# A trunk kernel whose mixer trips are reordered, with the residual's scaling on ScalarE

## The chip, the core and the metric

The kernel runs on one core of a Trainium2 chip. The metric is the device time of one execution in microseconds. Time before: 2114.56 us, the median of 3 runs (2111.04 to 2116.69).

## The reference, cut to what matters

Two decoder layers of 1024 tokens by 1024 channels in float32. Layer 0 has a pooling and gating mixer, layer 1 (the "odd" one) a short gated convolution. Each is followed by a residual, a layer norm, a feed-forward block of width 4096, another residual and norm, and a gated embedding.

```python
def short_conv_mixer(x, w_in, conv_w, w_out):
    proj = jnp.einsum('bsd,de->bse', x, w_in)
    gate_b, gate_c, h = jnp.split(proj, 3, axis=-1)
    z = gate_c * h
    zp = jnp.pad(z, ((0, 0), (CONV_WIDTH - 1, 0), (0, 0)))
    conv = sum(conv_w[k] * zp[:, k:k + s] for k in range(CONV_WIDTH))   # width 3
    return jnp.einsum('bse,ed->bsd', gate_b * conv, w_out)

x = layer_norm(DEEPNORM_ALPHA * x + mix, ln1_g[i], ln1_b[i])
```

## The kernel before, in words

Every product of float32 matrices is done as three matmuls of rounded parts (high by high, high by low, low by high), so each operand has to be split before: ScalarE copies the high part, GpSimd or VectorE subtracts it from the value for the low part. Large products are also done by a seven-product scheme on 2 x 2 quarters (Winograd's form of Strassen's scheme), so sums and differences of quarters are needed besides.

The order of the work is one list, made in `make_plan` (L338). Each engine walks through this list and does its own part of each stage, in order; semaphores join them. An instruction that waits thus holds all that stands behind it on its engine, and the same goes for SyncE, which issues nearly all DMAs.

The odd layer's mixer is laid out by `short_conv` (L558). Its parts, in order:

- Slab "c" and slab "h": the first 256 channels of gate_c and of h, by plain products. Each slab's weights lie in four pieces in `raw`, are loaded by SyncE and split (`split_high` on ScalarE, `split_low` on GpSimd, L1246). The split of slab "h" is part of stage "c". While TensorE works on "c", the second half of the tokens is turned and split. GpSimd can start with the trips' operands only after the slab, and the weights of the first trip (`w1_raw`) are loaded where `raw` lay, once it is split. At the end of stage "h" (L2168) VectorE forms z = c * h and does the convolution of block 0: four quarters by three operations.
- Ten trips, each of seven products (A11, S1, S2, A12, S4, S3, A22) of 12 matmuls: block 0 of gate_b, then for each of the blocks 1 to 3 the trips c, h and b. A22 of a trip is done within the next one, behind its S1; the last trip has S3 ahead of S4. The operand of step i + 4 is made during step i: sums S1 and S3 by VectorE (L1903, L1906), S2 and S4 by GpSimd (L1326, L1333), high parts by ScalarE (L1525), low parts by GpSimd (L1260). GpSimd makes the low parts of S1 and of S2 only when it comes to S2 and S4 of its own order.
- `od_evictions` (L1734) is VectorE's reading of the products: names such as c22 (final sum of a quarter), m22 (z's quarter, gated), g22 (the mixer's value), h1 to h4 (sums of quarters for the product with w_out). `od_conv` (L1713) is the convolution of one quarter: a scaling by the third tap, then two multiply-adds, each waiting for the one before. Before, two quarters follow S4 and two follow A22 of each trip h. TensorE may enter A22 only once S3's sum (L1787) is formed from the same bank.
- `od_copies` (L1409) is ScalarE's part. `od_loads_and_spills` (L1044) issues the weights' loads, writes the b trips' values to memory (`spill_g`), and `load_od_item` (L995) reads them back.
- 14 items: the product of the mixer's values with w_out, seven forms of two items of 24 matmuls each. An item is prepared (`prep`, L1483 and L1984) by splitting its values (hop) and its weights (wop). VectorE makes weight sums (`wsum`, L1955) where a form needs them, one item ahead. After the second item of a form VectorE adds the banks to the residual (L2010, L2013); the next form that uses the same banks waits for it.
- The residual is scaled by 4 ** 0.25 in eight pieces, one in each of eight trips, by GpSimd (stage "alpha", L1289).

Of the kernel before, what the change touches and what calls it, by code (L numbers as in the profile page):

```python
# [63 lines left out]
OD_HOP_AT = (184, 192, 48, 52, 128, 132, 200, 48, 52, 128, 132, 200, 48, 52)  # L64
OD_W_AT = (188, 196, 32, 36, 168, 172, 176, 180, 184, 188, 32, 36, 168, 172, 176, 180, 32, 36)
OD_STEPS = dict(
    c=dict(S1=("s15",), A22=("c21",), S2=("u1",), A12=(), S4=("c12",), S3=("c22",)),
    h=dict(S1=("s15",), A22=("c21", "m21", "v100", "v101", "v102", "v110", "v111", "v112"), S2=("u1",), A12=("m11",),
           S4=("c12", "m12", "v000", "v001", "v002", "v010", "v011", "v012"), S3=("c22", "m22")),
    b=dict(S1=("s15",), A22=("c21", "g21", "h4"), S2=("u1",), A12=("g11",), S4=("c12", "g12"),  # L70
           S3=("c22", "g22", "h1", "h2", "h3")))
OD_LAST = dict(OD_STEPS["b"], S3=("c22", "g22"), S4=("c12", "g12", "h1", "h2", "h3"))
# [81 lines left out]
class Ahead:  # L154


    def __init__(self, layer, after, items, pairs, joined):
        self.layer, self.items, self.pairs, self.joined = layer, items, pairs, joined
        n = len(items)
# [3 lines left out]
        self.act = [base["act"] + 2 * i + 2 for i in range(n)]  # L163
        self.first_load = [sum(len(FORMS[form][2]) for form, _ in items[:i]) for i in range(n)]
        loads = sum(len(FORMS[form][2]) for form, _ in items)
        dve, taken = base["dve"], base["taken"]
        self.sum, self.hop_low, self.dve, self.taken = [None] * n, [], [], []
        for i in range(-1, n):
            if i + 1 < n:
                dve += FORMS[items[i + 1][0]][3]  # L170
                self.sum[i + 1] = dve
            if i >= 0:
                self.hop_low.append(dve + 1)
                dve += 2
                self.dve.append(dve)
                taken += items[i][1] < pairs - 1 and not (joined and i == n - 2)
                self.taken.append(taken)
        self.total = dict(act=base["act"] + 2 * n, dve=dve, taken=taken, pool=base["pool"] + pairs,
                          hop=base["hop"] + n, load=base["load"] + loads)

# [72 lines left out]
class Trips:  # L253
# [6 lines left out]
    def __init__(self, layer, after, end):  # L260
# [19 lines left out]
        for b, op in self.seq:  # L280
# [8 lines left out]
            if layer == OD:  # L289
                kind = OD_TRIPS[b - PLAIN][0]  # L290
                for name in (OD_STEPS[kind] if b < end - 1 else OD_LAST).get(op, ()):
                    self.step[b, name] = len(self.step) + 1
# [5 lines left out]
            if op in self.QUARTER:  # L298
                self.quarter[b, self.QUARTER[op]] = layer * 4 * blocks + len(self.quarter) + 1
        self.total = dict(ops=base["ops"] + n, sums=base["sums"] + 2 * blocks, moves=base["moves"] + blocks,  # L300
                          loads=base["loads"] + blocks // 2)

# [2195 lines left out]
```

## Time and profile before

| | us |
|---|---|
| median of 3 runs | 2114.56 (2111.04 to 2116.69) |
| the profiled execution | 2113.19 |
| its span, first to last instruction | 2111.6 |
| TensorE busy | 2067.5 (98%) |
| VectorE busy | 1328.9 (63%) |
| ScalarE busy | 835.3 (40%) |
| GpSimd busy | 810.8 (38%) |

The mixer of the odd layer lies from 1000 to 1350 us. Matmuls overlap, so the time of one row (391 ns) is longer than the distance from one start to the next. The number in brackets behind an instruction is how long its engine stood idle before it, and what ended that.

### The profile page before, as it was taken

The numbers are of one execution on the slowest core, as the hardware profiler recorded it, in microseconds if no ns is written. First come the engines' busy times: TensorE is split into PE (matmuls) and PEld (weight loads), VectorE is DVE, ScalarE is ACT, GpSimd is POOL, SyncE is SP. The second block draws the span as 40 slices with busy tenths as digits, with TensorE's granted clock in tenths as the row PEclk, the third lists the DMA queues.
The fourth block names the chain that finished last, engine by engine and source line by source line (L and its number), as shares of the span: only waits on it lengthen the run. The fifth ranks groups of instructions, "written<-read, shape, count | busy, mean of one in ns | idle before, by whom it ended". The sixth has DMA issues, their size and how long they took to land. (4 is left out here: it accounts for less than half of the span.)

```text
span 2111.6 us, 25132 instructions
## 1 busy us (share of the span) xinstructions
PE 2067.5 (98%) x9437; PEld 1712.4 (81%) x9437; DVE 1328.9 (63%) x1689; ACT 835.3 (40%) x1215; POOL 810.8 (38%) x533
## 2 busy tenths in 40 slices
PE   9999999999999999999899997999999999999999
PEld 9888788888888888888777776888888888888887
DVE  4744775556666666565567757676565566666663
ACT  3112554544544335531322223554544543334530
POOL 5113167777512000230666650157777512000220
PEclk9999999999999999999999998999999999999999
DMA  5111024434599554310022229024444499554221
GB/s 186 41 60 55 26 80 155 151 139 160 189 366 376 199 189 160 110 56 15 20 96 88 72 76 340 28 81 151 142 146 164 177 366 387 184 196 170 95 85 40
DMA packets 191252, 307.10 MB, mean 145 GB/s; under 512 B 13504, under 2 KB 71964, under 8 KB 191132
## 3 DMA queue, kind: packets, MB, share of 16 engines
q1 hardware_dynamic: 190432, 305.19, 41.7%
q8 instruction: 75, 1.23, 0.2%
q14 instruction: 45, 0.37, 0.1%
q10 hardware_dynamic: 700, 0.31, 0.1%
HBM read 234.14 MB, written 71.30 MB: 145 GB/s over the span
## 5 line engine op out<-in xcount | busy, mean ns | idle before, releaser
L1246 POOL TENSOR_TENSOR w_lo<-raw,w_hi 128x512 fp32r<-128x512 f32 x92 | 140.7, 1561 | 736.3 <-ACT w_hi L1354 736.3
L1495 ACT CAST hop_hi<-h_raw 128x1024 fp32r<-128x1024 f32 x126 | 132.5, 1051 | 290.7 <-PE bank_a L2234 165.3
L1525 ACT CAST op_hi<-op_sum 128x512 fp32r<-128x512 f32 x152 | 94.5, 622 | 369.8 <-POOL op_sum L1333 97.6
L1260 POOL TENSOR_TENSOR op_lo<-op_sum,op_hi 128x512 fp32r<-128x512 f32 x152 | 222.5, 1480 | 42.6 <-ACT op_hi L1525 36.6
L2232 PE MATMUL bank_a<-wop_hi,hop_hi 128*128 128x512 f32 x576 | 225.3, 391 | 8.0 <-DVE resid L2010 8.0
L1988 DVE TENSOR_TENSOR hop_lo<-h_raw,hop_hi 128x1024 fp32r<-128x1024 f32 x126 | 154.4, 1226 | 121.8 <-ACT hop_hi L1495 121.5
L2234 PE MATMUL bank_a<-wop_hi,hop_lo 128*128 128x512 f32 x576 | 225.0, 391 | 0.0
L2233 PE MATMUL bank_a<-wop_lo,hop_hi 128*128 128x512 f32 x576 | 225.0, 391 | 0.0
L1260 POOL TENSOR_TENSOR op_lo<-w_raw,op_hi 128x512 fp32r<-128x512 f32 x114 | 165.0, 1447 | 120.5 <-ACT op_hi L1525 119.1
L2232 PE MATMUL bank_a<-xt_hi,op_hi 128*128 128x512 f32 x456 | 178.3, 391 | 1.8 <-DVE b L1752 1.8
L2233 PE MATMUL bank_a<-xt_lo,op_hi 128*128 128x512 f32 x456 | 178.1, 391 | 0.0
L2234 PE MATMUL bank_a<-xt_hi,op_lo 128*128 128x512 f32 x456 | 178.0, 390 | 0.0
L2232 PE MATMUL bank_b<-wop_hi,hop_hi 128*128 128x512 f32 x432 | 169.5, 392 | 3.2 <-DVE wop_lo L1991 3.2
L2234 PE MATMUL bank_b<-wop_hi,hop_lo 128*128 128x512 f32 x432 | 168.8, 391 | 0.0
L2233 PE MATMUL bank_b<-wop_lo,hop_hi 128*128 128x512 f32 x432 | 168.8, 391 | 0.0
L2232 PE MATMUL bank_a<-xt_hi,w_hi 128*128 128x512 f32 x320 | 127.6, 399 | 6.4 <-POOL w_lo L1246 6.4
L2232 PEld LDWEIGHTS bank_a<-wop_hi,hop_hi 128*128 128x128 f32 x576 | 108.8, 189 | 30.8 <-DVE wop_lo L1991 8.4
L1991 DVE TENSOR_TENSOR wop_lo<-w_raw,wop_hi 128x1024 fp32r<-128x1024 f32 x108 | 132.6, 1228 | 0.6
L2233 PEld LDWEIGHTS bank_a<-wop_lo,hop_hi 128*128 128x128 f32 x576 | 108.8, 189 | 22.7
L2234 PEld LDWEIGHTS bank_a<-wop_hi,hop_lo 128*128 128x128 f32 x576 | 108.7, 189 | 22.8
L1287 POOL TENSOR_TENSOR w_raw<-w_raw,w_raw 128x1024 f32<-128x1024 f32 x18 | 44.3, 2461 | 213.7 <-DMA w_raw<-in_ffn_w_dram 181.2
L2232 PE MATMUL bank_b<-t_hi,op_hi 128*128 128x512 f32 x304 | 120.4, 396 | 5.0 <-POOL op_lo L1260 4.9
(239 smaller groups left out, 4970.1 us busy)
## 6 DMA issues: line engine op xcount, KB each, us to landing
w_raw<-in_ffn_w_dram SPq DMA_DIRECT2D x144, 512.0 KB, 6.8
h_raw<-h_spill SPq DMA_DIRECT2D x112, 512.0 KB, 5.5
h_spill<-h_tile SPq DMA_DIRECT2D x170, 256.0 KB, 2.2
w_raw<-in_ffn_w_dram SPq DMA_DIRECT2D x112, 256.0 KB, 3.3
w_raw<-in_od_w_in_dram SPq DMA_DIRECT2D x40, 256.0 KB, 3.4
w_raw<-in_od_w_out_dram SPq DMA_DIRECT2D x18, 512.0 KB, 6.7
raw<-in_ple_gate_w_dram SPq DMA_DIRECT2D x32, 256.0 KB, 3.5
h_spill<-h_tile2t SPq DMA_DIRECT2D x28, 256.0 KB, 2.0
```

The lines of the kernel that those rows point to most:

```text
L1246: pool.tensor_tensor(lo, raw[:, n % NRAW, :], hi.bitcast(F32), ALU.subtract).then_inc(lo_split, 1)
L1260: pool.tensor_tensor(by_four(op_lo[s]), by_four(src) if src is not None else w1_quarter(b, op), by_four(op_hi[s]).bitcast(F32), ALU.subtra ...
L1287: pool.tensor_tensor(w2_chunk(a, i), w2_chunk(a, i), w2_chunk(a, i, 1), ALU.subtract)\
L1495: act.copy(hop_hi[k][:, :, :], h_raw[a.hop_chunk(i)][:, :, :]).then_inc(ahead_hi, 1)
L1525: act.copy(by_four(op_hi[s]), src).then_inc(op_high, 1)
L1988: dve.tensor_tensor(hop_lo[k][:, :, :], h_raw[a.hop_chunk(i)][:, :, :], hop_hi[k][:, :, :].bitcast(F32), ALU.subtract).then_inc(ahead_dve, 1)
L1991: dve.tensor_tensor(wop_lo[k][:, :, :], w2_source(a, i), wop_hi[k][:, :, :].bitcast(F32), ALU.subtract).then_inc(ahead_dve, 1)
L2232: pe.matmul(dst, s_hi, m_hi, start=first, stop=False, skip_group_check=on_top)
L2233: pe.matmul(dst, s_hi, m_lo, start=False, stop=False, skip_group_check=on_top)
L2234: return pe.matmul(dst, s_lo, m_hi, start=False, stop=last, skip_group_check=on_top)
```

## The change

Slab "h" is split by a stage of its own ("split") at the start of the mixer, ahead of the turned units. The convolution of a quarter keeps two operations on VectorE; the first, the scaling by the third tap, is done by ScalarE (`last_tap`). The four quarters' convolutions are spread over the steps S4 of trip h and A11, S2 and A12 of trip b; those of block 0 lie in the first trips and no longer in stage "h". The sums h2 and h3 and their writing to memory go to step A11 of the next trip. The last block's g11 and g21 are not written to memory: items 2 and 3 read them from their tiles, with two pieces of a copy and of a subtraction each. Items 1, 2 and 3 are loaded earlier (at S1 and S3 of the last trip), from other places. In the mixer a weight sum is made right before its own item (`sum_lead` false). "alpha" is ScalarE's in the mixer's trips.

```diff
-OD_HOP_AT = (184, 192, 48, 52, 128, 132, 200, 48, 52, 128, 132, 200, 48, 52)
-OD_W_AT = (188, 196, 32, 36, 168, 172, 176, 180, 184, 188, 32, 36, 168, 172, 176, 180, 32, 36)
+OD_HOP_AT = (184, 48, 52, 192, 128, 132, 200, 48, 52, 128, 132, 200, 48, 52)
+OD_W_AT = (188, 32, 36, 196, 168, 172, 176, 180, 184, 188, 32, 36, 168, 172, 176, 180, 32, 36)
+OD_DIRECT = {2: "g11", 3: "g21"}
...
-        if n + 1 < len(ahead[layer].items):
+        if not ahead[layer].sum_lead:
+            add("wsum", item=n, layer=layer)
+        elif n + 1 < len(ahead[layer].items):
             add("wsum", item=n + 1, layer=layer)
         add("prep", item=n, layer=layer)
...
     def short_conv():
         tr, a = trips[OD], ahead[OD]
+        add("split")
         turn = turns("gate", 1, list(range(KT)), ring="B", nested=True)
-        add("c", slab=("od", D), half=0, paced=True, split_next=True, inner=[turn])
+        add("c", slab=("od", D), half=0, paced=True, split_next=False, inner=[turn])
...
-                elif i == 1:
-                    sp.wait_ge(od_step, tr.step[last - 1, "v112"])
-                elif i in (2, 3):
+                elif i in (1, 2):
                     sp.wait_ge(trip_done, tr.done[last, "A11"])
+                elif i == 3:
+                    sp.wait_ge(od_step, tr.step[last, "v102"])
...
                 if (b, op) == (last, "A11"):
                     load_od_item(0)
-                if (b, op) == (last - 1, "A22"):
+                if (b, op) == (last, "S1"):
                     load_od_item(1)
-                if (b, op) == (last, "A12"):
                     load_od_item(2)
+                if (b, op) == (last, "S3"):
+                    load_od_item(3)
                 if (b, op) == (last, "S4"):
                     load_od_item(4)
                 if (b, op) == (last, "A22"):
-                    for n in (3, 5, 6):
-                        load_od_item(n)
+                    load_od_item(5)
+                    load_od_item(6)
...
+                def last_tap(k, half):
+                    c = ROW_CONV + 2 * KT + blk * BT + k
+                    act.activation(cv_at(k, half, blk), z_at(k, half), ACT.Copy, scale=cols[:, c:c + 1])\
+                        .then_inc(od_tap, 1)
+
+                if kind == "h" and op == "S4":
+                    act.wait_ge(od_step, tr.step[b, "m11"])
+                    last_tap(0, 0)
+                if kind == "h" and op == "S3":
+                    act.wait_ge(od_step, tr.step[b, "m12"])
+                    last_tap(0, 1)
...
+                if kind == "b" and blk and op == "A11":
+                    act.wait_ge(od_step, tr.step[b - 1, "m22"])
+                    last_tap(1, 1)
+                if kind == "b" and blk and op == "S2":
+                    act.wait_ge(od_step, tr.step[b - 1, "m21"])
+                    last_tap(1, 0)
...
+                    if a.parts(i) == 2:
+                        act.copy(hop_hi[k][:, 0, :], h_raw[a.hop_chunk(i)][:, 0, :]).then_inc(ahead_hi, 1)
+                        act.wait_ge(od_step, trips[OD].step[trips[OD].end - 1, OD_DIRECT[i]])
+                        act.copy(hop_hi[k][:, 1, :], kept_of(i)).then_inc(ahead_hi, 1)
...
+                if st.kind == "alpha" and st.layer == OD:
+
+                    half = st.turned[st.tiles[0] // HT]
+                    act.wait_ge(sem_of[half[0]], half[1])
+                    for t in st.tiles:
+                        act.activation(resid[:, t, :], resid[:, t, :], ACT.Copy, scale=ALPHA).then_inc(acc_ready, 1)
...
-                dve.tensor_scalar(d, z_at(k, half), taps[2], None, ALU.mult).then_inc(od_step, 1)
-                od_wait(b, name + "0")
+                dve.wait_ge(od_tap, 4 * blk + {(0, 0): 1, (0, 1): 2, (1, 1): 3, (1, 0): 4}[k, half])
                 dve.scalar_tensor_tensor(out=d, in0=z_at(k, half, 1), scalar=taps[1], in1=d, op0=ALU.mult, op1=ALU.add)\
                     .then_inc(od_step, 1)
...
+                if op == "A11":
+                    if kind == "c" and blk == 1:
+                        od_conv(b - 1, 0, 1, 0)
+                    if kind == "c":
+                        od_other_sums(b - 1)
+                    if kind == "b":
+                        od_conv(b, blk, 0, 1 if blk else 0)
...
                     if kind == "h":
                         od_wait(b, "c12")
                         dve.tensor_tensor(q12, q12, cv_12[:, :], ALU.mult).then_inc(od_step, 1)
-                        od_wait(b, "m12")
-                        od_conv(b, blk, 0, 0)
-                        od_conv(b, blk, 0, 1)
+                        od_conv(b + 1, blk, 0, 0)
...
                     if kind == "h":
                         od_wait(b, "c21")
                         dve.tensor_tensor(q21, q21, cv_at(1, 0, blk), ALU.mult).then_inc(od_step, 1)
-                        od_wait(b, "m21")
-                        od_conv(b, blk, 1, 0)
-                        od_conv(b, blk, 1, 1)
```

## Rows read from the trace of the kernel before

**Rows 1.** The page: busy time, TensorE's granted clock in slices, one costliest group.
```profile
PE 2067.5 (98%) x9437; PEld 1712.4 (81%) x9437; DVE 1328.9 (63%) x1689; ACT 835.3 (40%) x1215; POOL 810.8 (38%) x533
...
PEclk9999999999999999999999998999999999999999
...
L1246 POOL TENSOR_TENSOR w_lo<-raw,w_hi 128x512 fp32r<-128x512 f32 x92 | 140.7, 1561 | 736.3 <-ACT w_hi L1354 736.3
```

**Rows 2.** Waits of TensorE, whole span: us in total, times, longest.
```profile
PE bank_a L2232 <- DVE resid L2010: 8.0, 1, 8.0
PE bank_b L2232 <- DVE z L1787: 6.6, 3, 3.1
PE bank_a L2232 <- POOL w_lo L1246: 6.4, 1, 6.4
PE bank_b L2232 <- POOL op_lo L1260: 4.9, 10, 3.4
PE bank_a L2232 <- POOL op_lo L1260: 3.9, 3, 1.8
PE bank_b L2232 <- DVE wop_lo L1991: 3.2, 1, 3.2
PE bank_a L2232 <- DVE b L1752: 1.8, 1, 1.8
```

**Rows 3.** Windows of 50 us: busy (x instructions) by engine, granted clock, DMA.
```profile
400.00:450.00 50.00, 49.83 (x220) 40.83 (x220) 32.63 (x35) 22.89 (x41) 40.66 (x28) 1.00 0.43 153
...
1050.00:1100.00 50.00, 46.33 (x196) 37.37 (x195) 38.42 (x42) 12.23 (x20) 29.36 (x20) 0.97 0.31 101
...
1300.00:1350.00 50.00, 44.03 (x183) 36.27 (x184) 42.01 (x63) 23.93 (x30) 8.19 (x5) 0.90 0.49 173
```

**Rows 4.** Timelines around slab "h": start, us, engine, line, operation.
```profile
941.28 10.48 SPq L933 DMA_DIRECT2D raw<-in_od_w_in_dram  x8
...
1009.40 0.92 DVE L1666 CAST xt_hi<-t_raw 128x512 fp32r<-128x512 f32 x2 [5.91 <-ACT t_raw L1405]
...
1015.88 12.28 POOL L1246 TENSOR_TENSOR w_lo<-raw,w_hi 128x512 fp32r<-128x512 f32 x1 [64.52 <-ACT w_hi L1354]
...
1032.91 0.63 PE L2234 MATMUL bank_a<-xt_hi,w_lo 128*128 128x512 f32 x1
```

**Rows 5.** Timelines, first trip b: VectorE behind S4 of h, TensorE at A22.
```profile
1114.87 1.40 DVE L1717 TENSOR_SCALAR cv<-z,cols 128x512 f32<-128x512 f32 x1
1116.31 0.75 DVE L1719 SCALAR_TENSOR_TENSOR cv<-z,cols,cv 128x512 f32<-128x512 f32 x1
1117.09 1.66 DVE L1722 SCALAR_TENSOR_TENSOR cv<-z,cols,cv 128x512 f32<-128x512 f32 x1
...
1124.20 0.79 PE L2232 MATMUL bank_b<-xt_hi,op_hi 128*128 128x512 f32 x1 [3.13 <-DVE z L1787]
```

**Rows 6.** Groups of instructions, 1000 to 1345 us; ScalarE's from 1340 to 1420.
```profile
L1722 DVE SCALAR_TENSOR_TENSOR cv<-z,cols,cv 128x512 f32<-128x512 f32 x12 | 14.4, 1200 | 0.4
...
L1294 POOL TENSOR_SCALAR resid<-resid 128x1024 f32<-128x1024 f32 x8 | 10.0, 1256 | 0.7
...
L1402 ACT ACTIVATE t_raw<-bank_b,cols 128x512 f32<-128x512 f32 x4 | 2.9, 779 | 0.4 <-PE bank_b L2271 0.4
```

**Rows 7.** Timelines, last trip: VectorE's S3 sum, TensorE at S2.
```profile
1248.74 0.68 DVE L1906 TENSOR_TENSOR op_sum<-w_raw 128x512 f32<-128x512 f32 x1
...
1254.55 0.77 PE L2232 MATMUL bank_b<-t_hi,op_hi 128*128 128x512 f32 x1 [3.38 <-POOL op_lo L1260]
```

**Rows 8.** Waits of SyncE's DMA queue, 1225 to 1325 us.
```profile
SPq L1017 <- DVE cv L1722: 20.1, 1, 20.1
```

**Rows 9.** Timelines, items 4 to 6: GpSimd's weight difference, VectorE's additions.
```profile
1292.42 2.36 POOL L1287 TENSOR_TENSOR w_raw<-w_raw,w_raw 128x1024 f32<-128x1024 f32 x1 [8.96 <-DMA w_raw<-in_od_w_out_dram]
...
1305.15 2.47 DVE L2010 TENSOR_TENSOR resid<-resid,bank_a 128x512 f32<-128x512 f32 x4
...
1317.92 2.46 DVE L2010 TENSOR_TENSOR resid<-resid,bank_a 128x512 f32<-128x512 f32 x4
```

More of the change, by code:

```diff
@@ L158, in __init__ @@
         self.layer, self.items, self.pairs, self.joined = layer, items, pairs, joined
+        self.sum_lead = layer != OD
         n = len(items)
@@ L172, in __init__, with parts @@
             if i >= 0:
-                self.hop_low.append(dve + 1)
-                dve += 2
+                if not self.sum_lead:
+                    dve += FORMS[items[i][0]][3]
+                    self.sum[i] = dve
+                self.hop_low.append(dve + self.parts(i))
+                dve += self.parts(i) + 1
                 self.dve.append(dve)
+                act += self.parts(i) + 1
+                self.act.append(act)
                 taken += items[i][1] < pairs - 1 and not (joined and i == n - 2)
                 self.taken.append(taken)
-        self.total = dict(act=base["act"] + 2 * n, dve=dve, taken=taken, pool=base["pool"] + pairs,
+        self.total = dict(act=act, dve=dve, taken=taken, pool=base["pool"] + pairs,
                           hop=base["hop"] + n, load=base["load"] + loads)
+    def parts(self, i):
+        return 2 if self.layer == OD and i in OD_DIRECT else 1
     def user_before(self, i):
@@ L301, in __init__, with gate_trip, od_names, conv @@
                           loads=base["loads"] + blocks // 2)
+    @staticmethod
+    def gate_trip(blk):
+        return PLAIN + OD_TRIPS.index(("b", blk))
+    def od_names(self, b, op):
+        kind, blk = OD_TRIPS[b - PLAIN]
+        last = b == self.end - 1
+        names = [(b, n) for n in dict(S1=("s15",), A22=("c21",), S2=("u1",), S4=("c12",), S3=("c22",)).get(op, ())]
+        def conv(owner, k, half):
+            names.extend((owner, f"v{k}{half}{tap}") for tap in (1, 2))
+        if kind == "c" and op == "A11":
+            if blk == 1:
+                conv(b - 1, 1, 0)
+            names += [(b - 1, "h2"), (b - 1, "h3")]
+        if kind == "h":
+            names += [(b, n) for n in dict(A22=("m21",), A12=("m11",), S4=("m12",), S3=("m22",)).get(op, ())]
+            if op == "S4":
+                conv(b + 1, 0, 0)
+        if kind == "b":
+            names += [(b, n) for n in dict(A22=("g21", "h4"), A12=("g11",), S4=("g12",), S3=("g22",)).get(op, ())]
+            if op == "A11":
+                conv(b, 0, 1 if blk else 0)
+            if op == "S2":
+                conv(b, 1 if blk else 0, 1)
+            if op == "A12":
+                conv(b, 1, 0 if blk else 1)
+            if op == ("S4" if last else "S3"):
+                names += [(b, n) for n in (("h1", "h2", "h3") if last else ("h1",))]
+        return names
     def slot_before(self, j):
@@ L1059, in od_loads_and_spills @@
                 if kind == "b":
-                    if op == "A12":
+                    if op == "A12" and b < last:
                         spill_g(b, 0, "g11", cv_11)
```

127 lines of the change are left out of this document (70 added, 57 removed).

## The prediction

> **What bounds the kernel now.** I read the busy shares first: TensorE 98% of the span, no other engine above 63% [rows 1]. A gain must therefore come out of TensorE's waits, or out of time in which it runs at its lower clock. In the 40 slices of 52.8 us its granted clock is 9 everywhere but in one, the 25th (1267 to 1320 us), which lies in the odd layer's mixer (1000 to 1350 us). Second, the waits of TensorE: three of the big ones are the mixer's [rows 2]: 8.0 us for the residual's addition (L2010), 6.4 us for the split of a weight slab by GpSimd (L1246), 6.6 us in three waits for VectorE's addition L1787; the 3.2 us for wop_lo, the 1.8 us for L1752 and, of the op_lo waits, the three of bank_a (1.8, 1.1 and 1.0) and the longest of bank_b (3.4) lie there too. Together 8.0 + 6.4 + 6.6 + 3.2 + 1.8 + 3.9 + 3.4 = 33.3 us of idle time. Third, windows [rows 3]: an undisturbed stretch holds 220 matmuls in 49.83 busy us, 0.2265 us each. The six windows from 1050 to 1350 hold 1150 in 300 us, which is 260.5 us of work: 39.5 us lost. The slab's wait stands before them: 6.4 us idle, and after it matmuls start 0.42 us apart, 7 of them, 1.5 us more [rows 4]. Whole loss in the mixer: 47.4 us, 33.3 idle and about 14 of restarts and of running at the lower of the two clocks (1.2 instead of 2.4 GHz, starts 0.43 us apart). This is the ceiling of what a new order can give.
>
> **The slab's split.** It is moved from behind the turned units (stage "c") to the mixer's start. Its data is there since about 955 us (issued from 941.28), yet GpSimd begins it at 1015.88, and its first subtraction takes 12.28 us, because VectorE then runs two-input operations back to back [rows 4]; the mean over all 92 is 1.56 [rows 1]. Moved, it starts when the gate's last bank is full, about 1000.8, VectorE is busy until 1003.5 and then idle for 5.9 us, to 1009.4 [rows 4], so four subtractions end by 1003.5 + 4 x 1.5 = 1009.5, before the 1025.3 at which TensorE wants the slab. The Trainium skill says (SBUF — State Buffer, "SBUF: two separate sides") that a GpSimd operation and a VectorE one with two SBUF inputs lock a port pair whole, the later one blocked; the 12.28 us agree. By it, too, the early place is free of the block after 1003.5. Gone: 6.4 + 1.5 + 0.1 = 8.0 us. The weights behind it (w1, whose buffer lies on raw) come 20 us earlier, so the next operands are not late: GpSimd then has some 15 us of work in 21.8 us of matmuls.
>
> **The convolution in the trips.** Before, an "h" trip runs 6 operations (2 quarters x 3 taps) on VectorE at S4 and 6 at A22; block 0 has 12 in front of the first trip. Ahead of L1787, which TensorE needs to enter A22, stand six of them [rows 5]. After, the first tap's product is ScalarE's (16 operations, the nearest row a 128x512 scaling with columns as scale and bias, 779 ns [rows 6]), and the remaining 8 VectorE operations of a block lie in four stages, two each. Alone one takes 0.75 us, beside GpSimd 1.66 [rows 5]. In trip b of block 1: the six begin at 1114.87; two operations at 1.66 in their place end at 1118.2, then L1787 1118.9; TensorE wants it at 1120.9. Margin 2 us, wait of 3.1 us gone with its slow clock. The same in block 2, and 0.3 in block 3. The next operand sum (S1 of trip c) is now computed at about 1130 in place of 1136.4 less the 4.9 of the lost wait; its chain to TensorE takes 6.9 us, needed at 1137.2: the 1.0 and 1.1 us go, leaving 0 to 0.7. For block 0 the 12 operations no longer stand ahead of the first sums, so the 1.8 us for L1752 and its slow clock go; the 1.8 us of op_lo shrinks: VectorE reaches the S1 sum 13.2 us into the trip (taps, s15, the fourth operand's low part, u1, two operations), plus 6.3 is 19.5, wanted 19.0: 0.5 kept.
> Work put in front of others: a ScalarE tap waits for a gated product and holds the operand casts behind it. ScalarE's cast for the step is issued first, its idle times there are 2 to 8 us, and it is busy 40% [rows 1]; I take zero, bound 0 to 0.6 us a trip. The sums h2, h3 and their spills go one step later, behind 1 MB of weights in the queue; VectorE's S2 waits for that landing 5 us later. Zero.
>
> **The scaling.** 8 operations of 128x1024, 1.26 us each on GpSimd; on ScalarE an estimate of 1.6 at most, twice the 779 ns of half the size [rows 6]. None stands directly ahead of a TensorE wait. Worth 0, bounds -0.5 and +1.
>
> **The last trip keeps its wait.** There TensorE wants S2 before GpSimd has it, because the S3 sum goes first in GpSimd's order: VectorE's sum starts at 1248.74, S2's product at 1254.55, 5.8 us later, 3.4 idle [rows 7]. The change leaves this order. The sum starts earlier only by what leaves VectorE's queue: two-tap pairs (1.66, 1.66, 0.8, 0.8) for six operations of 5.8, 0.9 us, of which the lost 0.3 us wait takes back some. I keep 3.2 idle + 2.8 slow clock (12 to 14 starts at 0.43) + 0.1 = 6.1 us.
>
> **The products.** Items 1 to 3 are loaded up to 20 us earlier (item 1's load was held for 20.1 us by a convolution [rows 8]); the last block's g11 and g21 are split straight from their tiles, 1 MB less to move, and the 5.4 us of landing before item 3 go. So the 3.2 us wait for wop_lo and its 1.8 us slow clock go. The 8.0 us wait shrinks but doesn't go: VectorE's additions of m1 stand behind the preparations of items 5 and 6. GpSimd starts item 5's weight difference at 1292.42 when its data land, and the additions start at 1305.15, 12.7 us later [rows 9]. After: in microseconds from the last trip's start, VectorE issues h4's value at 34, item 5's loads follow and land at 42 (4.3 MB since 30, at the 390 GB/s of that stretch), difference 44.4, weight sum 45.6, item 5 48.0, item 6 51.5, first addition 52.2. TensorE wants item 4 at 49.5: 2.8 us. The additions for m6 come 12.8 us behind those for m1 (1317.92 less 1305.15 [rows 9]), first bank 13.4: at 64.9 against a wanted 60.4. So 4.5 us in both, a slow clock of up to 1.7 us hidden in it.
>
> **Sum.** Lost now 47.4. Kept: 0.5 (block 0), 0.6 (blocks 1 and 2), 6.1 (last trip), 4.5 (products) = 11.7. Gain 35.7 us. The profiled execution took 2113.19 (span 2111.6), so 2077.5; the median of the runs is 1.4 above it, 2078.8. I take 2078. The rest of the program is untouched, with some 6 us of waits in all.
>
> **Rivals.** First, the contention rival: each pair of convolution operations runs beside GpSimd (1.66 + 1.66), and GpSimd is held by VectorE in turn, as in the 12.28 us. Then the margins of 2.0 and 0.3 us are gone and each of four trips b waits 1.5 us, at the lower clock for 1.6 more, and the products 2 us: 14.4, thus 2092. For it: the mean of L1722, 1.20 us against 0.75 alone [rows 5, 6]. Against: there are a third fewer such operations, and the scaling has left GpSimd. The page named above says the pair is held for the whole instruction, which is what this rival needs. Second, the last wait and the additions come on time as well: 6.1 and 4.5 go, 2068. Against it is the fixed order on GpSimd. Third, slower: ScalarE as the choke. Its taps, waiting on VectorE, hold the casts, GpSimd and TensorE in a ring. It decides only if more than 35.7 + 6.3 us are lost in four trips b, 10.5 each: 2120. Against: taps take under 3 us a block and their inputs are ready one step before. Fourth, the change doesn't do what it says: the waits only move to operand loads and the gain is under 6 us, 2110.
>
> **How the numbers follow.** Forecast (2070 to 2086) 0.56; contention (2086 to 2100) 0.23; all waits gone (2062 to 2070) 0.15; nothing gained 0.03; slower 0.03. Below 2064 lie some 0.04, above 2094 some 0.14, so 2064 to 2094 for 8 in 10. Faster by over 0.3% (6.3 us, about what a measurement of this kernel tells from no change) 0.95, within 0.02, slower 0.03.
>
> **What the profile would show.** GpSimd's first L1246 of the slab at 1001 to 1009 and no wait in the middle of the slabs; no wait of over 1 us for L1787's successor in trips b; the one for op_lo in the last trip still at about 3 us; one of 2 to 4 us for the residual's addition, and perhaps a second, at the third form. Wrong would be: VectorE's two-tap pairs at 3.3 us throughout, a last trip without wait, or item 4 waiting over 6 us.

## The result and the profile after

The changed kernel takes 2078.03 us, the median of 4 runs (2077.88 to 2078.84), against 2113.57 (2111.04 to 2116.69, 4 runs) for the kernel before: ratio 0.9832, 95% interval 0.9815 to 0.9849. The profiled execution took 2077.88 (span 2076.2), 35.3 us less than the profiled one of before. Of the runs further down one is left out of its median, 2855.95 us at a mean granted clock of 0.675 (slab split late; 0.995 to 0.996 in the other three).

Lines have moved: the matmuls of a product are L2322 to L2324, the residual's additions L2110 and L2113 (L2010 and L2013 before), the slab's low parts L1298 (L1246), the operands' low parts L1312 (L1260), VectorE's two multiply-adds of a convolution L1802 and L1805, ScalarE's product L1490, the sum ahead of A22 L1880 (L1787).

The page of the changed kernel (busy time by engine, then TensorE's granted clock in 40 slices), to be laid beside [rows 1]:

```profile
PE 2054.6 (99%) x9437; PEld 1704.6 (82%) x9437; DVE 1320.0 (64%) x1675; ACT 853.7 (41%) x1241; POOL 795.5 (38%) x525
...
PEclk9999999999999999999999999999999999999999
```

TensorE's waits, whole span (us in total, times, longest), to be laid beside [rows 2]:

```profile
PE bank_a L2322 <- DVE resid L2110: 5.2, 1, 5.2
PE bank_b L2322 <- POOL op_lo L1312: 4.5, 10, 3.0
PE bank_a L2322 <- POOL op_lo L1312: 1.7, 2, 1.4
```

Four lines of [rows 2] have no successor: the slab's (6.4), the sum ahead of A22 (6.6), wop_lo (3.2) and L1752 (1.8). The 8.0 of the residual is 5.2. Of the 4.5 in bank_b, 2.95 is one wait, the last trip's. The windows of 50 us (busy and instructions by engine, granted clock, share of DMA), to be laid beside [rows 3]:

```profile
1050.00:1100.00 50.00, 48.31 (x213) 39.35 (x212) 35.02 (x38) 19.33 (x31) 32.72 (x23) 1.00 0.27 89
1100.00:1150.00 50.00, 50.00 (x222) 41.42 (x221) 37.65 (x38) 17.02 (x28) 36.34 (x26) 1.00 0.30 100
1150.00:1200.00 50.00, 50.00 (x222) 41.38 (x222) 38.17 (x39) 18.31 (x29) 34.81 (x24) 1.00 0.28 91
1200.00:1250.00 50.00, 47.05 (x208) 38.65 (x207) 31.57 (x40) 19.50 (x28) 19.27 (x15) 1.00 0.37 128
1250.00:1300.00 50.00, 44.77 (x188) 36.51 (x187) 40.76 (x49) 19.34 (x22) 13.47 (x7) 0.93 0.82 296
```

From 1100 to 1200 us TensorE never stops. The clock falls below 1.00 in one window only, at the products.

What is left is five waits. TensorE's rows that begin after a wait or at the lower clock (start, us, operation, idle time and its releaser):

```profile
1067.24 0.47 PE L2322 MATMUL bank_a<-t_hi,op_hi 128*128 128x512 f32 x1 [1.35 <-POOL op_lo L1312]
...
1228.87 0.47 PE L2322 MATMUL bank_b<-t_hi,op_hi 128*128 128x512 f32 x1 [2.95 <-POOL op_lo L1312]
1229.17 0.40 PE L2323 MATMUL bank_b<-t_lo,op_hi 128*128 128x512 f32 x1
...
1269.75 0.76 PE L2322 MATMUL bank_a<-wop_hi,hop_hi 128*128 128x512 f32 x1 [5.23 <-DVE resid L2110]
1270.31 0.63 PE L2323 MATMUL bank_a<-wop_lo,hop_hi 128*128 128x512 f32 x1
...
1316.22 0.47 PE L2322 MATMUL bank_b<-wop_hi,hop_hi 128*128 128x512 f32 x1 [0.26 <-DVE resid L2113]
```

Behind the wait of 2.95 matmuls start 0.24 us apart; behind that of 5.23 twelve start 0.43 us apart, the lower level of 1.2 GHz. A start of that kind is called slow below. Counting what each start takes beyond 0.2265 us, the waits cost 1.7 (block 0), 0.6 (the trip behind it, 0.34 idle), 3.2 (last trip), 5.4 + 2.5 of slow clock = 7.9 (the fifth item, which the kernel counts as item 4) and 0.5 (ahead of m4): 13.9 us kept. Counted in the same way, the kernel before loses 49.2 us between slab "h" and the last product, 33.4 of it idle, so restarts and slow clock were nearer 16 than the forecast's "about 14". The difference, 49.2 less 13.9, is the 35.3 between the two executions.

### The profile page after: what moved, and what is told of

The parts are those of the page before. It is cut to its first block and busy times, and to the rows that moved or that the text cites. A ratio compares the mean times of both kernels' runs of the same rounds, so it can differ in the third digit from the quotient of the medians.

```text
span 2076.2 us, 25147 instructions
## 1 busy us (share of the span) xinstructions
PE 2054.6 (99%) x9437; PEld 1704.6 (82%) x9437; DVE 1320.0 (64%) x1675; ACT 853.7 (41%) x1241; POOL 795.5 (38%) x525
## 3 DMA queue, kind: packets, MB, share of 16 engines
q8 instruction: 75, 1.23, 0.3%
## 5 line engine op out<-in xcount | busy, mean ns | idle before, releaser
L1298 POOL TENSOR_TENSOR w_lo<-raw,w_hi 128x512 fp32r<-128x512 f32 x92 | 130.9, 1455 | 717.6 <-ACT w_hi L1406 717.5
L1312 POOL TENSOR_TENSOR op_lo<-op_sum,op_hi 128x512 fp32r<-128x512 f32 x152 | 226.3, 1504 | 36.3 <-ACT op_hi L1609 30.3
L2322 PE MATMUL bank_a<-wop_hi,hop_hi 128*128 128x512 f32 x576 | 225.2, 391 | 5.2 <-DVE resid L2110 5.2
L2324 PE MATMUL bank_a<-wop_hi,hop_lo 128*128 128x512 f32 x576 | 225.0, 391 | 0.0
L1312 POOL TENSOR_TENSOR op_lo<-w_raw,op_hi 128x512 fp32r<-128x512 f32 x114 | 162.5, 1425 | 117.7 <-ACT op_hi L1609 116.6
L2324 PE MATMUL bank_a<-xt_hi,op_lo 128*128 128x512 f32 x456 | 177.4, 389 | 0.0
L2322 PE MATMUL bank_a<-xt_hi,op_hi 128*128 128x512 f32 x456 | 177.4, 389 | 0.0
L2322 PE MATMUL bank_b<-wop_hi,hop_hi 128*128 128x512 f32 x432 | 168.8, 391 | 0.3 <-DVE resid L2113 0.3
L2324 PE MATMUL bank_b<-wop_hi,hop_lo 128*128 128x512 f32 x432 | 168.2, 389 | 0.0
L2322 PEld LDWEIGHTS bank_a<-wop_hi,hop_hi 128*128 128x128 f32 x576 | 108.8, 189 | 28.3 <-DVE wop_lo L2091 5.6
L2324 PEld LDWEIGHTS bank_a<-wop_hi,hop_lo 128*128 128x128 f32 x576 | 108.7, 189 | 22.7
L2322 PE MATMUL bank_a<-xt_hi,w_hi 128*128 128x512 f32 x320 | 126.8, 396 | 0.0
L2324 PE MATMUL bank_a<-xt_hi,w_lo 128*128 128x512 f32 x320 | 124.7, 390 | 0.0
L2323 PE MATMUL bank_a<-xt_lo,w_hi 128*128 128x512 f32 x320 | 124.6, 389 | 0.0
```

What stands on the lines that cost most here:

```text
L1298: pool.tensor_tensor(lo, raw[:, n % NRAW, :], hi.bitcast(F32), ALU.subtract).then_inc(lo_split, 1)
L1312: pool.tensor_tensor(by_four(op_lo[s]), by_four(src) if src is not None else w1_quarter(b, op), by_four(op_hi[s]).bitcast(F32), ALU.subtra ...
L2322: pe.matmul(dst, s_hi, m_hi, start=first, stop=False, skip_group_check=on_top)
L2323: pe.matmul(dst, s_hi, m_lo, start=False, stop=False, skip_group_check=on_top)
L2324: return pe.matmul(dst, s_lo, m_hi, start=False, stop=last, skip_group_check=on_top)
```

## Experiments

All times stand beside runs of the kernel before on the same chip, and the ratio is to those; the ratio to compare with is the changed kernel's 0.9832. The kernel before took 2113.57 us beside the changed kernel and 2114.32 to 2116.53 beside the experiments, so a difference of medians and one of ratios can be up to 3 us apart. Where they are, both are given, as bounds.

**The early split alone.** The kernel before, with only the slab's split moved.

```diff
+        add("split")
         turn = turns("gate", 1, list(range(KT)), ring="B", nested=True)
-        add("c", slab=("od", D), half=0, paced=True, split_next=True, inner=[turn])
+        add("c", slab=("od", D), half=0, paced=True, split_next=False, inner=[turn])
```

> The kernel before with one part of the change alone: slab h is split at the mixer's start. Theory (the waits of the mixer add up, each with its own cause): the 6.4 us wait for L1246 and the 1.6 us of slow clock and restart behind it go and nothing else moves, so 8.0 us off the 2113.6 of before: 2105.6, between 2104 and 2107. Rival (the early split only moves the wait, to the first trip's operands, since GpSimd has 15 us of other work in front of it): 2110 to 2114.

Measured: 2106.88 us (2104.12 to 2108.99), ratio 0.9956 (0.9941 to 0.9971), within the expected range. TensorE's waits in the mixer:

```profile
PE bank_a L2233 <- DVE resid L2011: 8.0, 1, 8.0
PE bank_b L2233 <- DVE z L1788: 6.6, 3, 3.1
PE bank_a L2233 <- DVE b L1753: 3.6, 1, 3.6
PE bank_b L2233 <- POOL op_lo L1261: 3.4, 1, 3.4
PE bank_b L2233 <- DVE wop_lo L1992: 3.2, 1, 3.2
PE bank_a L2233 <- POOL op_lo L1261: 2.2, 3, 1.0
```

The slab's wait is gone, and all others stand as they were but two: L1753 (L1752 before) waited 1.8 and now waits 3.6, and the three for op_lo in bank_a, the first of them right behind it, wait 2.2 in place of 3.9. TensorE comes 8 us sooner to the first trip, where VectorE still has block 0's twelve convolution operations in front of what it needs. So 1.8 us were pushed from one wait of block 0 to another, and nothing came on top. By the ratio this part is worth 9.3 us (6 to 12); counted by starts, the mixer of the profiled execution loses 41.1 us in place of 49.2.

**The early split undone in the changed kernel.** The same edit the other way.

> The changed kernel with one part undone: slab h is split again at the end of stage c, as before. My theory: GpSimd begins at about 1015 us beside VectorE's back-to-back additions, its first subtraction takes about 12 us, TensorE waits 6.4 us for the slab with 1.5 us of lower clock behind it, and the first weights of the trips come 20 us later, which with the new order of block 0's convolution costs 0 to 2 us more: 2086 to 2088, 0.4% slower than the changed kernel. Rival: the early split was worth more in the changed kernel than alone (the additions of block 0 stand in the first trips now, where GpSimd's late start would cut their margins): 2090 to 2095.

Measured: 2087.44 us, the median of three runs (2086.93 to 2088.94), ratio 0.9872 (0.9856 to 0.9889). GpSimd and TensorE at the slab:

```profile
1015.94 15.96 POOL L1297 TENSOR_TENSOR w_lo<-raw,w_hi 128x512 fp32r<-128x512 f32 x4 [64.51 <-ACT w_hi L1405]
...
1031.95 0.79 PE L2321 MATMUL bank_a<-xt_hi,w_hi 128*128 128x512 f32 x1 [6.42 <-POOL w_lo L1297]
...
1037.66 0.60 PE L2322 MATMUL bank_a<-xt_lo,w_hi 128*128 128x512 f32 x1
```

9.4 us by the medians (8.5 by the ratios), where 8 to 10 were expected. In the profiled execution the wait and the slow clock behind it cost 9.6: 14 matmuls start 0.43 us apart, where the kernel before had 7 behind a wait of the same 6.42 us (8.1 in all). Block 0's waits are less (0.64 and 0.35 in place of 1.35 and 0.34), and so is the fifth item's (4.96, with 8 slow starts: 1.1 us less). The last trip costs 1.6 more: its wait is of the same length, 2.93 against 2.95, but here seven matmuls start 0.43 us apart from 1.5 us behind it on.

```profile
1238.14 0.47 PE L2321 MATMUL bank_b<-t_hi,op_hi 128*128 128x512 f32 x1 [2.93 <-POOL op_lo L1311]
...
1239.69 0.63 PE L2321 MATMUL bank_b<-t_hi,op_hi 128*128 128x512 f32 x1
```

**The residual's scaling back on GpSimd.**

```diff
-                if st.kind == "alpha" and st.layer == OD:
...
-                        act.activation(resid[:, t, :], resid[:, t, :], ACT.Copy, scale=ALPHA).then_inc(acc_ready, 1)
...
-                if st.kind == "alpha" and st.layer != OD:
+                if st.kind == "alpha":
```

> The kernel after with the residual's scaling back on GpSimd, 8 operations of 1.26 us. Theory: none stands directly ahead of a wait of TensorE, worth 0: 2078.0, within 0.7. Rival (the port pair shared by GpSimd and VectorE is what counts): each of the 8 holds VectorE or a low part for up to 1.3 us and some of that reaches TensorE: 2080 to 2084.

Measured: 2078.37 us (2077.37 to 2080.45), ratio 0.9823 (0.9809 to 0.9838), as expected, with the same waits to a tenth (5.2, 2.9, 1.4, 0.3). What differs in its trace is seven slow starts behind the last trip's wait, 1.5 us, where the changed kernel's execution has none. This part is worth nothing that can be told from nothing.

**The first products back on VectorE, in the new places.**

```diff
-                if kind == "h" and op == "S4":
-                    act.wait_ge(od_step, tr.step[b, "m11"])
-                    last_tap(0, 0)
...
+                dve.tensor_scalar(d, z_at(k, half), cols[:, c:c + 1], None, ALU.mult).then_inc(od_tap, 1)
...
```

> The kernel after with the convolution's first product (16 operations) back on VectorE, in the new places. Theory (the spreading is what removes the waits, the move to ScalarE adds little): in trips b of blocks 1 and 2 S3's sum keeps most of its 2 us of margin (one more operation of 0.5 to 1.4 us), only the last trip's wait grows by some 1 to 2 us: 2078.5 to 2081. Rival (the margins are thin, the move to ScalarE carries the gain): waits of 1 to 2 us with a slow clock in four trips, 2084 to 2092.

Measured: 2084.27 us (2082.39 to 2085.13), ratio 0.9847 (0.983 to 0.9863). The mixer's waits:

```profile
PE bank_a L2309 <- DVE resid L2097: 5.0, 1, 5.0
PE bank_b L2309 <- POOL op_lo L1312: 4.1, 1, 4.1
PE bank_a L2309 <- POOL op_lo L1312: 3.7, 3, 2.7
```

6.2 us more than the changed kernel by the medians, 3.2 by the ratios, whose intervals overlap (the two kernels' runs don't). That is more than was expected, and at the edge of the rival's range, but not by the rival's mechanism. The even spreading alone nearly holds the margins of the trips (two waits of 0.5 us, at 1128 and 1186). The loss is at places that had waits already: block 0's goes from 1.35 to 2.73 and is followed by 14 slow starts, the last trip's from 2.95 to 4.07, with 8; the fifth item's is 4.96, with 13. Without the 0.3 ahead of m4 waits are 12.8 us in place of 9.9, slow clock is 7.3 in place of 2.5. The expectation counted only the last trip's growth (1.1 us) and not block 0's (1.4). How many slow starts follow a wait varies from one execution to another (last section), so that of the 6.2 us the 2.9 of wait are shown to be the first products', the slow clock only in part.

**The convolution lumped again.** ScalarE keeps its products, but for blocks 1 to 3 they and all the rest stand in trip h as before: two quarters at S4, two at A22.

```diff
             if op == "S4":
                 conv(b + 1, 0, 0)
+                conv(b + 1, 0, 1)
+            if op == "A22":
+                conv(b + 1, 1, 0)
+                conv(b + 1, 1, 1)
```

> The kernel after with the first products on ScalarE, but in blocks 1 to 3 the rest of the convolution in its old places: two quarters (four operations) behind S4 and two behind A22 of trip h. Theory (the spreading carries it): four operations of up to 1.66 us stand ahead of S3's sum, which ends 1.3 us too late in blocks 1 and 2; with the slow clock and a last trip that waits 1 to 3 us longer 2082 to 2089. Rival (the move to ScalarE carries it): 2078 to 2080.

Measured: 2081.80 us (2080.91 to 2082.48), ratio 0.9838 (0.9823 to 0.9853): 3.8 us slower by the medians and 1.3 by the ratios, less than was expected and more than the rival had. The waits for the sum ahead of A22 don't come back; two of 0.9 us for the low part of S1 in the next trips do. So taking a third of the operations out of the queue of [rows 5] is enough for A22, and the spreading is needed for what is behind it. In the trace these two waits cost 2.1 us with their restarts; another 1.5 are seven slow starts behind the last trip's wait, which is as long as the changed kernel's (2.94). With the run before: the two halves of the convolution's change are worth 3 to 6 us (ScalarE's products) and 1 to 4 us (the places), each given the other.

**Items 2 and 3 by way of memory, with the late loads.**

```diff
-OD_DIRECT = {2: "g11", 3: "g21"}
+OD_DIRECT = {}
...
-                if (b, op) == (last, "S1"):
+                if (b, op) == (last, "A12"):
                     load_od_item(1)
                     load_od_item(2)
-                if (b, op) == (last, "S3"):
-                    load_od_item(3)
                 if (b, op) == (last, "A22"):
+                    load_od_item(3)
                     load_od_item(5)
```

> The kernel after with the last block's g11 and g21 written to memory and read back as before, and items 1 to 3 loaded late (items 1 and 2 at A12, item 3 at A22 of the last trip). Theory: item 3 waits for a landing again, some 3 us with 1.7 us of slow clock, and 1.5 MB more before item 5's weights put the residual's additions 2 to 4 us later: 2082 to 2087. Rival (the products are bound by the rows of VectorE's own work, not by loads): the wait at item 3 only replaces part of the one at item 4: 2078 to 2080.

Measured: 2086.08 us (2084.18 to 2087.35), ratio 0.987 (0.9855 to 0.9884), within the expected range.

```profile
1263.78 0.79 PE L2321 MATMUL bank_b<-wop_hi,hop_hi 128*128 128x512 f32 x1 [3.71 <-DVE wop_lo L2090]
...
1277.00 0.76 PE L2321 MATMUL bank_a<-wop_hi,hop_hi 128*128 128x512 f32 x1 [5.09 <-DVE resid L2109]
```

The wait for wop_lo is back (3.7 beside 3.2 in [rows 2]), with its slow clock, and the one for the residual stays what it was. Slow clock is 6.5 us in all (31 starts, 6 of them behind the last trip's unchanged wait) in place of 2.5. The direct tiles and the early loads together are worth 8 us, 3.7 of it wait; no run parts the two.

**Weight sums an item ahead, as before.**

```diff
-        self.sum_lead = layer != OD
+        self.sum_lead = True
```

> The kernel after with the weight sums of the mixer's items made one item ahead again. Theory: VectorE waits for item 5's weights before it makes item 4's low parts and has one more sum ahead of the additions (item 7's, 1.14 us), while the pair of item 4's low parts (2.3 us) moves behind GpSimd's difference: item 4's wait grows by 3.4 us, the additions for m6 come 2.3 us later: 2080.5 to 2082. Rival (loads set it): no change, 2078.0 within 0.7.

Measured: 2079.64 us (2077.79 to 2081.77), ratio 0.984 (0.9825 to 0.9855). VectorE's additions of m1 come later, TensorE's wait before the fifth item is 7.5 us in place of 5.2, 2.3 more, where 3.4 more were expected. The time grows by 1.6 by the medians, less than the expected 2.5 to 4 and not clear of the noise (the runs of the two kernels overlap). In the traces there are 1.8 us of slow clock behind the longer wait and 2.5 behind the shorter one, and the wait of 0.3 before m4 is gone.

**The last trip's order on GpSimd.** In the last trip GpSimd makes the sum for S4 and the low part of S2 ahead of the low part of S3.

```diff
+            if layer == OD and b == end - 1:
+                lows = {"S1": (), "S2": ("S1",), "S3": ("S2", "S3")}
...
+                        elif (tr.layer, b, op) == (OD, tr.end - 1, "S3"):
+                            pool.tensor_tensor(by_four(op_sum[s]), w1_quarter(b, "A12"), by_four(s2), ALU.subtract)\
+                                .then_inc(sum_by_pool, 1)
+                            operand_low(tr, b, "S2")
+                            operand_low(tr, b, "S3")
```

> The kernel after with another order on GpSimd in the last trip alone: the S4 sum and S2's low part go ahead of S3's low part, so that S2 doesn't wait for VectorE's S3 sum. Theory (this order is the whole cause of the 2.95 us wait): it shrinks to about 0.4 us. The products' chain hangs partly on this trip's ends: gain 2 to 3 us, 2075 to 2076. Rival (the products' chain hangs on loads): the wait only moves to item 4, which then waits 2.5 us longer: 2078.0 within 0.7.

Measured: 2074.96 us (2074.18 to 2075.67), ratio 0.9816 (0.98 to 0.9833), 3.1 us faster than the changed kernel, as expected. GpSimd in the changed kernel, then in this one:

```profile
1224.53 1.29 POOL L1312 TENSOR_TENSOR op_lo<-op_sum,op_hi 128x512 fp32r<-128x512 f32 x1 [4.72 <-ACT op_hi L1609]
1225.79 1.26 POOL L1385 TENSOR_TENSOR op_sum<-w_raw,op_sum 128x512 f32<-128x512 f32 x1
1227.13 2.84 POOL L1312 TENSOR_TENSOR op_lo<-op_sum,op_hi 128x512 fp32r<-128x512 f32 x2
```

```profile
1223.69 1.62 POOL L1389 TENSOR_TENSOR op_sum<-w_raw,op_sum 128x512 f32<-128x512 f32 x1 [3.47 <-PE bank_a L2338]
1225.39 4.24 POOL L1315 TENSOR_TENSOR op_lo<-op_sum,op_hi 128x512 fp32r<-128x512 f32 x3
```

The wait of 2.95 is 0.49. That it came from GpSimd's fixed order, as [rows 7] was read, is thereby shown.

**The additions ahead of the preparations.** In the changed kernel VectorE's additions of m1 stand behind the preparing of the items up to 6 (counted from 0). Here no more than item 4 is prepared before them, and items 5 to 7 before those of m2 and m6.

```diff
-            while nxt < len(OD_ITEMS) and (a.user_before(nxt) is None or a.user_before(nxt) < i):
+            cap = {1: 4, 2: 4, 3: 7, 4: 7, 5: 7}.get(i, len(OD_ITEMS))
+            while nxt < len(OD_ITEMS) and nxt <= cap and (a.user_before(nxt) is None or a.user_before(nxt) < i):
```

> The kernel after with the residual's additions for m1 ahead of the preparations of items 5 and 6, and those for m6 ahead of items 8 and 9. Theory (the additions are late because of what stands ahead of them on VectorE): the additions start at about 1259.5, as item 2 ends, item 4 starts at its own time, 1264.4: 5.2 us idle and 2.5 us of slow clock go, 2070 to 2072. Rival (item 5's weights, landing at 1258.9, set the pace): the wait moves to item 5 or 6, of 3 to 5 us: 2074 to 2078.

Measured: 2078.99 us (2078.77 to 2081.39), ratio 0.9839 (0.9825 to 0.9854): no gain, where 6 to 8 us were expected, and not the rival either. The wait moved:

```profile
PE bank_b L2323 <- DVE resid L2114: 4.8, 1, 4.8
...
PE bank_a L2323 <- DVE resid L2111: 0.5, 1, 0.5
```

The fifth item waits 0.5, and 7.4 us of wait and slow clock are gone there; but TensorE then waits 4.84 us at 1315.67 ahead of m4, which goes into the bank that m7 has just filled. VectorE (and, in the first row, ScalarE) in front of that:

```profile
1310.97 1.28 ACT L1695 ACT_TABLE_LOAD   x1
...
1310.99 0.17 DVE L2191 TENSOR_SCALAR var_eps<-squares 128x4 f32<-128x4 f32 x1 [2.76 <-ACT unread L1689]
...
1313.39 1.53 DVE L1912 TENSOR_SCALAR resid<-resid,neg_mean,rstd 128x1024 f32<-128x1024 f32 x2
1314.84 0.68 DVE L2114 SCALAR_TENSOR_TENSOR resid<-resid,bank_b 128x512 f32<-128x512 f32 x1
```

VectorE ends m3's additions at 1308, waits 2.76 us for ScalarE's squares and 1.3 for its root, normalizes, and only then adds m7, all of which TensorE had finished by about 1310.8, when it fell idle. In the changed kernel the same chain stood there and cost 0.26 us, since TensorE came 5 us later.

**Both edits.**

> The changed kernel with two of the earlier edits at once: in the last trip GpSimd makes the sum for S4 and the low part of S2 ahead of the low part of S3, and the preparing of items 5 to 8 on VectorE is held back behind the additions of the first two forms. My theory after the run with the additions first: the wait in front of item 4 only moves to the fourth item from the end, because VectorE's additions of m7 stand behind the first half's layer norm, and that behind m3's additions, whose time is set by VectorE's own queue. TensorE arrives there 3 us earlier still, so the new wait grows by these 3 us, and the gain of the first edit is lost as well: 2076 to 2079. Rival: the two gains add up (2078.0 - 3.1 - up to 7.7 us): 2067 to 2072.

Measured: 2075.19 us (2074.37 to 2076.94), ratio 0.9816 (0.9799 to 0.9832). The additions again bring nothing, as expected (2074.96 without them); but the 3.1 of the other edit are kept, which I had thought lost. The wait ahead of m4 is 5.12 and not 8: the chain itself came earlier, m7's first addition at 1309.22 in place of 1314.84. VectorE's last wait ahead of m3's additions is the one for GpSimd's weight difference, and behind it the queue runs on without a gap to 1302.4:

```profile
1252.17 1.23 DVE L2087 TENSOR_TENSOR t_od<-w_raw,w_raw 128x1024 f32<-128x1024 f32 x1 [2.38 <-POOL w_raw L1343]
```

In the run before, the same row starts at 1258.03, 5.9 us later, and m7's first addition comes 5.6 later. GpSimd in turn had waited for the item's weights, whose loads are issued in the last trip. So the chain is a fixed stretch behind that trip's steps, not a fixed time, and most of it is VectorE's own queue. 2.5 of the 5.9 us are the wait that the other edit took away; 2.9 are slow starts behind it, 14 in the trace of the run before and none here.

**Both edits, and the first half's norm behind m7.**

```diff
             if OD_ITEMS[i] == ("m3", OD_PAIRS - 1):
                 squares_of(lo)
+            if OD_ITEMS[i] == ("m7", OD_PAIRS - 1):
                 add("stats", half=0, ln=2)
                 add("norm", half=0, ln=2)
```

> The same two edits, and besides the first half's statistics and layer norm stand on each engine behind the second item of m7, so that VectorE adds m7's banks to the residual before it normalizes. If the chain m3's additions, norm, m7's additions is what took the gain back, the wait of 4.8 us in front of the first item of m4 goes or falls under 2 us (m3's additions end at about 1308, m7's first bank could then be free by 1309, TensorE wants it at about 1307.5): 2067 to 2071. Rival: VectorE's own load in this stretch is the bound (the preparations of four items from 1284 to 1304.7, stretched beside GpSimd), so the wait stays over 3 us, or the normalized tiles come late for the turned units and the wait only moves there: 2073 to 2078.

Measured: 2067.20 us (2066.70 to 2071.49), ratio 0.9779 (0.9764 to 0.9795), 10.8 us faster than the changed kernel, 46 faster than the one before. VectorE now adds m7's banks one by one, each as it is full:

```profile
1306.10 0.69 DVE L2129 SCALAR_TENSOR_TENSOR resid<-resid,bank_b 128x512 f32<-128x512 f32 x1 [0.35 <-PE bank_b L2340]
...
1307.46 0.69 DVE L2129 SCALAR_TENSOR_TENSOR resid<-resid,bank_b 128x512 f32<-128x512 f32 x1 [0.66 <-PE bank_b L2340]
```

TensorE doesn't wait ahead of m4 at all, and 0.2 us at the turned units behind it. The profiled execution is the slowest of the four (2071.49; the others 2066.7 to 2067.3). It has a wait of 2.5 us at the fifth item that the run before didn't have (0.5):

```profile
PE bank_a L2338 <- DVE resid L2126: 2.5, 1, 2.5
...
1256.07 3.35 DVE L2107 TENSOR_TENSOR wop_lo<-t_od,wop_hi 128x1024 fp32r<-128x1024 f32 x1
```

There a subtraction of VectorE's took 3.35 us beside a GpSimd difference that had begun at 1255.75, 0.3 us ahead of it. In the run before, VectorE's began 0.07 us ahead of GpSimd's (1254.52 and 1254.59) and took 1.23. Whether this overlap is what divides the one execution from the other three stays open, since those have no trace.

## Why the prediction was right, and where only by luck

The forecast was 2078.0, measured is 2078.03. The mechanism held in the main: the waits that were to go went, those that were to stay stayed, and undoing a part, the scaling aside, brought waits back or made them longer. The exact hit is luck, by errors that cancel: 11.7 us were to be kept and 13.9 were (block 0 and m4 1.7 more, the products 3.4 more, the last trip 2.9 less), while the loss of before, put at 47.4, was 1.8 larger. Of the signs that it named, one missed: the wait for the residual's addition was to be 2 to 4 us, with perhaps a second, and was 5.2 without one.

- **The slab's split: right.** GpSimd's first subtraction starts at 1000.98 (forecast 1000.8) and no wait is left. The end was 1007.5, 2 us before the forecast's 1009.5, and there was a price that was not counted: VectorE still had three operations to do, and they were stretched (the last two rows; 0.42 and 0.68 us are those of the same operations alone, and the first, a cast, has one input).

```profile
1000.98 6.55 POOL L1298 TENSOR_TENSOR w_lo<-raw,w_hi 128x512 fp32r<-128x512 f32 x4 [50.00 <-ACT w_hi L1406]
...
1001.48 1.52 DVE L1750 CAST xt_hi<-tmp 128x512 fp32r<-128x512 f32 x1
1002.92 3.47 DVE L1755 TENSOR_TENSOR xt_lo<-tmp,xt_hi 128x512 fp32r<-128x512 f32 x2
```

  Before, VectorE held GpSimd for 12.28 us [rows 4]; here both advance by turns. The Trainium skill (SBUF — State Buffer, "SBUF: two separate sides") has the later of the two blocked for the other's whole instruction; the trace agrees with 1.7 us for each of VectorE's 0.68. The two runs on this part give 9.3 us (alone) and 8.5 to 9.4 (undone), beside the 8.0 of the sum, which had 7 slow starts behind the wait.
- **Block 0: mis-sized.** 0.5 us forecast, 1.7 measured. L1752's wait went as said, and S1 of the next trip waits 1.35 for its low part. VectorE came to its sum 13.8 us into the trip (forecast 13.2), and its low part was ready 6.6 us later (6.3), at 20.4 against a wanted 19.0, which the forecast had right.
- **The trips b: right.** No wait from 1100 to 1200 us. The sum ahead of A22 in the trip from 1103.35 ends at 1106.7, wanted at 1108.8: a margin of 2.1, forecast 2.0. The pair took 1.78 + 1.66, as priced from [rows 5]; GpSimd, held in turn as the contention rival had it, still gave the low parts in time. The price of 3.4 a pair, which the forecast named as a sign against itself if it held throughout, held in 6 of the 16 pairs; the others took 1.5 to 2.6. VectorE's rows, and last ScalarE's:

```profile
1102.64 1.78 DVE L1802 SCALAR_TENSOR_TENSOR cv<-z,cols,cv 128x512 f32<-128x512 f32 x1
1104.45 1.66 DVE L1805 SCALAR_TENSOR_TENSOR cv<-z,cols,cv 128x512 f32<-128x512 f32 x1
1106.04 0.67 DVE L1880 TENSOR_TENSOR z<-z,bank_b 128x512 f32<-128x512 f32 x1
...
1102.78 0.72 ACT L1490 ACTIVATE cv<-z,cols 128x512 f32<-128x512 f32 x1
```

- **ScalarE as the choke: didn't come.** Its product takes 0.72 us (779 ns was the row taken) and no row of TensorE's waits names it. The Trainium skill's table of engines (Trainium Architecture — The Big Picture, "The five engines, in one table") advises against ScalarE for simple arithmetic, as up to about 3 times slower per element than VectorE. The traces show less: the same product took VectorE 0.48 to 1.52 us, and giving it to the slower but idle engine was worth 3 to 6 us.
- **The scaling: right**, 0 forecast, 0.3 with intervals that overlap widely measured.
- **The last trip: the wait right, the clock wrong.** 3.2 us idle forecast, 2.95 measured, out of GpSimd's order. But the 2.8 us of slow clock, copied from [rows 7], did not follow in the profiled execution. That is the error of −2.9, and it is a matter of the execution, not of the kernel: the run with the additions first is the same program up to this wait, and behind its 2.94 us fourteen starts are slow.

```profile
1228.16 0.76 PE L2323 MATMUL bank_b<-t_hi,op_hi 128*128 128x512 f32 x1 [2.94 <-POOL op_lo L1313]
1228.72 0.63 PE L2324 MATMUL bank_b<-t_lo,op_hi 128*128 128x512 f32 x1
```

- **The products: mis-sized, the additions' time met by luck.** From the last trip's start at 1217.59 the additions of m1 were forecast at +51.5 and came at +51.3, m6's 12.8 us behind and came 12.84 behind. TensorE, however, wanted the fifth item at +46.8, not +49.5: these are the 2.8 us of slow clock that didn't come. Hence 5.23 in place of 2.8 idle, with 2.5 of slow clock behind, 7.9 in place of 4.5 in all, and no second wait at m6's banks, since TensorE had lost its time already. It would be wrong to read from this that only the wanted time was off, for the additions don't stand at a fixed time behind the trip's start. In every run that keeps the order of the products they come later as the trip gets longer (us from the last trip's start, from the rows of each trace):

| run | last trip's wait, slow starts | fifth item wanted | additions start | wait |
|---|---|---|---|---|
| last trip's order | 0.49, 0 | 44.3 | 48.8 | 5.24 |
| changed kernel | 2.95, 0 | 46.8 | 51.3 | 5.23 |
| scaling on GpSimd | 2.93, 7 | 48.2 | 52.8 | 5.24 |
| convolution lumped | 2.94, 7 | 48.2 | 52.2 | 4.67 |
| slab split late | 2.93, 7 | 48.4 | 52.7 | 4.96 |
| products on VectorE | 4.07, 8 | 49.5 | 53.8 | 4.96 |

The distance is 4.0 to 4.6 us, and the wait 4.7 to 5.2 whatever the trip does. The term that was mis-sized is the chain from h4's value to the additions: forecast at 17.5 us (value at 34, landing at 42, additions at 51.5), it took 20.0 (value formed at 31.35, landing at 41.26, additions at 51.33):

```profile
1248.25 0.69 DVE L1903 TENSOR_TENSOR b<-cv,b 128x512 f32<-128x512 f32 x1
...
1258.85 2.98 POOL L1339 TENSOR_TENSOR w_raw<-w_raw,w_raw 128x1024 f32<-128x1024 f32 x1 [2.97 <-DMA w_raw<-in_od_w_out_dram]
...
1268.92 2.47 DVE L2110 TENSOR_TENSOR resid<-resid,bank_a 128x512 f32<-128x512 f32 x4
```

Most of it is the landing of item 5's data, 9.9 us in place of 8. With the forecast's slow clock in the last trip the whole would have come later and the time would have been some 2081, an estimate from the 2078 measured and the 2.8 that did not come.
- **What was not seen**: how near the next bound lay. The chain from m3's additions over the norm to m7's cost 0.26 us in the changed kernel and 4.84 as soon as TensorE came 5 us sooner. The rival "all waits gone, 2068" can't be had by the additions alone; it took the norm's place too (2067.2).

## What to carry to other kernels

Where a wait is priced by two times, the releaser's and the moment at which the engine wants it, ask first whether both hang on the same event: here both moved with the last trip's end, so the distance between them was the term to forecast, and a releaser met to 0.2 us still gave a wait off by 2.4. When a wait is removed, look along the same engine for the next instruction that stands in a queue behind foreign work (here additions behind a layer norm), since it will take the gain; move both or neither. And an idle engine that is slower at an operation may be the right place for it, if the fast one stands on the path.

## What the runs showed of the hardware

The drop of TensorE's clock follows neither from the length of the wait alone nor from the program. The last trip's wait was 2.93 to 2.96 us in seven traces, and the slow starts behind it were 0 (changed kernel), 0 (weight sums ahead), 14 (additions first), 7 (scaling on GpSimd), 7 (convolution lumped), 6 (items by memory) and 7 that began 1.5 us later (slab split late); the first and the third are the same program up to there. The slab's wait of 6.42 us had 7 behind it in the kernel before and 14 with the slab split late. Other waits: 2.73 and 4.07 (products on VectorE) with 14 and 8, 5.23 with 12, 7.5 with 8, which is 1.8 us of slow clock and less than the 2.5 behind the 5.23. A slow start is 0.43 us and not 0.2265. What decides how many a wait gets is open; for a forecast it is a term of 0 to 3 us for each wait near 3 us, and two traces that differ by less than that in slow clock say nothing about their kernels.

GpSimd and VectorE with two-input operations on 128x512 at once: the twelve-microsecond stall of [rows 4] came again when the split began amid VectorE's run of operations (15.96 us for four, with the late split), and not when VectorE had three left (6.55 for four); there VectorE paid as well, with 1.7 us for each 0.68.
